# Every block's output is multiplied by the gate as VectorE takes it from PSUM, and gathered rows are added straight into the input rows

## The reference, cut to what matters

```python
    h = rms_norm(x, norm2[l]) * (1.0 + sc2) + sh2
    x = x + g2 * moe_ffn(h, router_w[l], ...)
    return rms_norm(x, norm_f)

def moe_ffn(...):                      # rows sorted by expert into blocks of 128
    def expert_block(args):
        x_blk, e = args
        gu = x_blk @ w_gu[e] + b_gu[e]
        gate = jnp.minimum(gu[:, :D_FF], SWIGLU_LIMIT)
        up = jnp.clip(gu[:, D_FF:], -SWIGLU_LIMIT, SWIGLU_LIMIT)
        act = (up + 1.0) * (gate * jax.nn.sigmoid(SWIGLU_ALPHA * gate))
        return act @ w_down[e] + b_down[e]
    yb = lax.map(expert_block, (xb, block_e)).reshape(rows, D)
    y = jnp.zeros((N, D), h.dtype).at[stok].add(yb[dest] * sg[:, None].astype(h.dtype))
```

## Time and profile before

| | |
|---|---|
| median of three runs | 1630.07 us (1626.98 to 1631.4) |
| profiled execution, its own time | 1626.56 us |
| its span | 1624.6 us |
| busy: PE, DVE, ACT, POOL | 95%, 83%, 60%, 12% of the span |
| mixer and router | about the first 450 us |
| expert blocks | about 450 to 1595 us |
| end: last additions and norm | about 1595 to 1625 us |

### The profile page before, as it was taken

The page is one execution under the profiler, slowest core; times in us unless marked ns, Lnnn a source line. Parts: engine busy times, 40 slices in busy tenths (PEclk is TensorE's granted clock), DMA queues, the critical chain, the costliest instruction groups (busy, mean ns, idle before and its releaser), DMA issues.

```text
span 1624.6 us, 22048 instructions
## 1 busy us (share of the span) xinstructions
PE 1542.7 (95%) x8260; PEld 1163.2 (72%) x8260; DVE 1341.9 (83%) x1048; ACT 979.2 (60%) x787; POOL 187.9 (12%) x210
## 2 busy tenths in 40 slices
PE   3999989998699999999999999999999999999996
PEld 2444358845567787888888888888888888888873
DVE  5557447474878999999999999999999999999987
ACT  4013233311546776777777777777777777777772
POOL 1000121000001110100000100000110000010051
PEclk9999999998789999999999999999999999999998
DMA  9686020242369998999999999999999999999993
GB/s 377 254 343 236 29 91 29 69 168 110 143 258 347 339 390 335 381 388 390 388 380 383 381 380 387 396 391 376 387 379 387 386 395 385 377 388 377 375 379 123
DMA packets 85761, 506.81 MB, mean 312 GB/s; under 512 B 11008, under 2 KB 12336, under 8 KB 33360
## 3 DMA queue, kind: packets, MB, share of 16 engines
q1 hardware_dynamic: 70880, 453.85, 71.5%
q0 software_dynamic: 9104, 34.08, 5.8%
q10 hardware_dynamic: 5728, 18.18, 2.8%
HBM read 477.25 MB, written 28.84 MB: 312 GB/s over the span
## 4 chain that ended last, share of the span: by engine, by line
PE 87%; DVE 7%; DMA 2%; issue 2%; ACT 1%; POOL 1%; SPq 0%; DVEq 0%; POOLq 0%
PE ps L2067 61%; PE ps L1218 8%; PE ps L2083 2%; PE ps L1991 2%; PE ps L1295 2%; PE ps L1120 2%; PE ps L1224 2%; DVE w_lo L1474 2%; PE ps L2046 2%; DMA Wt<-in_ada_w 2%; PE ps L2056 1%; PE ps L1166 1%; PE ps L1193 1%; PE ps L1185 1%; PE ps L2089 0%
## 5 line engine op out<-in xcount | busy, mean ns | idle before, releaser
L1474 DVE TENSOR_TENSOR w_lo<-w_raw,w_hi 128x2048 fp32r<-128x2048 f32 x384 | 864.9, 2287 | 72.5 <-ACT w_hi L1468 72.4
L1468 ACT ACTIVATE w_hi<-w_raw 128x2048 fp32r<-128x2048 f32 x384 | 736.6, 1920 | 291.0 <-PE ps L2067 291.0
L2067 PE MATMUL ps<-w_hi,xTh 128*128 128x512 f32 x1024 | 408.3, 399 | 6.4 <-DVE w_lo L1474 5.8
L2067 PE MATMUL ps<-w_lo,xTh 128*128 128x512 f32 x1024 | 401.6, 392 | 0.0
L2067 PE MATMUL ps<-w_hi,xTl 128*128 128x512 f32 x1024 | 275.7, 391 | 0.0
L2067 PEld LDWEIGHTS ps<-w_hi,xTh 128*128 128x128 f32 x1024 | 194.6, 190 | 60.0 <-issue 16.5
L2067 PEld LDWEIGHTS ps<-w_hi,xTl 128*128 128x128 f32 x1024 | 193.4, 189 | 40.4
L2067 PEld LDWEIGHTS ps<-w_lo,xTh 128*128 128x128 f32 x1024 | 194.3, 190 | 38.5
L2067 PE MATMUL ps<-w_hi,aTh 128*128 128x512 f32 x512 | 202.4, 395 | 0.0
L2067 PE MATMUL ps<-w_lo,aTh 128*128 128x512 f32 x512 | 199.4, 389 | 0.0
L2067 PE MATMUL ps<-w_hi,aTl 128*128 128x512 f32 x512 | 157.6, 389 | 0.0
(11 more groups left out here) (396 smaller groups left out, 1372.3 us busy)
## 6 DMA issues: line engine op xcount, KB each, us to landing
w_raw<-in_moe_w_gu SPq DMA_DIRECT2D x256, 1024.0 KB, 6.6
w_raw<-in_moe_w_down SPq DMA_DIRECT2D x128, 1024.0 KB, 7.0
Wt<-in_ada_w SPq DMA_DIRECT2D x19, 1024.0 KB, 10.4
y_rows<-R ACTq DMA_DIRECT2D x30, 512.0 KB, 6.7
Wt<-in_w_in SPq DMA_DIRECT2D x5, 2048.0 KB, 13.4
y_rows<-Wt POOLq DMA_DIRECT2D x1, 8704.0 KB, 40.7
R<-in_ada_w SPq DMA_DIRECT2D x5, 1024.0 KB, 8.2
R<-in_x SPq DMA_DIRECT2D x2, 2048.0 KB, 10.3
```

The costliest lines, as they stand in the source:

```text
L1468: nc.scalar.activation(w_hi[:, at[-1] % HI_SLOTS, :], w_raw[:, at[-1] % RAW_SLOTS, :], ACT.Copy).then_inc(hi_rdy, 1)
L1474: nc.vector.tensor_tensor(w_lo[:, s, :], w_raw[:, s, :], w_hi[:, at[-1] % HI_SLOTS, :].bitcast(F32), ALU.subtract).then_inc(lo_rdy, 1)
L2067: ins = mm(ps[:, bank0 + c, :], x[:, k, :], w[:, 512 * (banks * i + c):512 * (banks * i + c) + 512], start=(first and i == 0 and x is xh a ...
```

## The change

1. **In the loop.** ACT no longer copies the output of block n-2 out of PSUM. A new function `y_scaled` on DVE, between low halves 3 and 4 of each step (from step 2 on), multiplies banks 6 and 7 by the gate into `ysb[s]`. ACT's `y_store` only waits for it and issues the DMA, in the place where it stood.
2. **Kept blocks.** `y_keep` moves to DVE and multiplies by the gate; for block 31 in two halves of 512 columns, between the adds of tiles 1 and 2. For that PE's last chunk (`last_chunk`) finishes bank 6 before bank 7, and PE's final additions wait per half.
3. **Rows.** As all outputs hold the gate already, `add_row` adds the weighted rows straight into `x2`, all four on DVE; ACT's first-row multiply is gone, and `total` is one addition.
4. **Small.** PE reads the overflow count ahead of the last chunks. ACT runs a one-element root ahead of the final squares. Some semaphores of the mixer and the router are merged (`y_cen` into `y_sum`, `var_mm` into `mean_mm`, `sat_rdy` into `gexp_rdy`, `tail_ev` into `gmt_rdy`).

```diff
-            def y_store(n, s, dn_end, stored, count=None):
-                wait_used(act, dn_end)
-                if stored is not None:
-                    act.wait_ge(y_out[s], 16 * stored)
-                s_.activation(ysb[s].rearrange("p (b c) -> p b c", b=2), ps[:, 6:8, :], ACT.Copy).then_inc(y_ev, 1)
+            def y_store(n, s, count=None):
                 act.wait_ge(y_ev, n + 1 if count is None else count)
                 act.dma_start(y_d[bass.ds(n * BLK, BLK), :], ysb[s]).then_inc(y_out[s], 16)
...
             split_hi(act, place(E, 0))
             split_hi(act, place(E, 1))
-            y_keep(0, place(E - 1, CHUNKS - 1))
             at_evac(E - 1)
             split_hi(act, place(E, 2))
             split_hi(act, place(E, 3))
-            for t in range(TT - 1):
-                act.wait_ge(yg_in[t], 16 * TOPK)
-                s_.activation(yg[t][0], yg[t][0], ACT.Copy, scale=gate_of[:, 0, t, 0:1]).then_inc(first_rdy, 1)
-            y_keep(1, place(E, 3))
...
+            s_.activation(fmx[:, 0:1], epsc[:], ACT.Sqrt)
...
+            def y_scaled(s, dn_end, stored):
+                wait_used(dve, dn_end)
+                if stored is not None:
+                    dve.wait_ge(y_out[s], 16 * stored)
+                v.tensor_tensor(two(ysb[s]), ps[:, 6:8, :], two(mod[5]), ALU.mult).then_inc(y_ev, 1)
+
+            def step(n, where, before, terms=(), done=0, out=None):
                 swiglu(n - 1, before(KT - 1))
                 x_lo(n)
                 for c in range(KT):
+                    if c == 4 and out is not None:
+                        y_scaled(out[0], before(CHUNKS - 1), out[1])
                     if c >= done:
                         split_lo(dve, where(c))
...
+            wait_used(dve, place(E - 1, CHUNKS - 1))
+            y_keep(0, 0, D)
             a_lo(E - 1)
             split_lo(dve, place(E, 2))
             split_lo(dve, place(E, 3))
...
+                return v.scalar_tensor_tensor(out=x2[:, t, :], in0=yg[t][k], scalar=gate_of[:, which, t, k:k + 1],
+                                              in1=x2[:, t, :], op0=ALU.mult, op1=ALU.add)
...
+            add_rows(0)
+            add_rows(1)
+            dve.wait_ge(half_mm, 1)
+            y_keep(1, 0, 512)
+            wait_used(dve, place(E, 3))
+            y_keep(1, 512, D)
+            add_rows(2)
...
-                b = 2 * t
-                if t < TT - 1:
-                    link(v.tensor_tensor(two(yg[t][0]), ps[:, b:b + 2, :], two(yg[t][0]), ALU.add))
-                    into_x(t).then_inc(x3_rdy, 1)
-                else:
-                    link(v.tensor_tensor(two(xg[0]), ps[:, b:b + 2, :], two(mod[5]), ALU.mult))
-                    v.tensor_tensor(x2[:, t, :], x2[:, t, :], xg[0], ALU.add).then_inc(x3_rdy, 1)
+                v.tensor_tensor(two(x2[:, t, :]), ps[:, 2 * t:2 * t + 2, :], two(x2[:, t, :]), ALU.add).then_inc(x3_rdy, 1)
```

More of the change, by code:

```diff
@@ L1636, in _, with step @@
                 split_hi(act, place(1, c))
[L1638 to L1642, removed]
+            def step(n, s, where, before, yn):
                 sigmoid(n - 1, before(KT - 1))
@@ L1647, in step @@
                 if yn is not None:
-                    y_store(yn, s, before(CHUNKS - 1), stored)
+                    y_store(yn, s)
                 for c in range(4, KT):
@@ L1858, in _ @@
             bias_down(0)
-            dve.wait_ge(sat_rdy, 1)
-            def step(n, where, before, terms=(), done=0):
+            dve.wait_ge(gexp_rdy, 3)
+            def y_scaled(s, dn_end, stored):
[4 more added lines that the diff above has]
+            def step(n, where, before, terms=(), done=0, out=None):
                 swiglu(n - 1, before(KT - 1))
@@ L1902, in _ @@
             step(1, at_step(1), at_step(0), ((1, 2), (2, 7)), EARLY)
-            step(2, at_step(2), at_step(1), ((3, 7),))
-            for n in (3, TT):
-                step(n, at_step(n), at_step(n - 1))
+            step(2, at_step(2), at_step(1), ((3, 7),), out=(0, None))
+            step(3, at_step(3), at_step(2), out=(1, None))
+            step(TT, at_step(TT), at_step(TT - 1), out=(0, 1))
             tail_rows()
@@ L1954, in _ @@
                 for t in range(TT - 1):
-                    link_over(v.tensor_scalar(yg[t][0], yg[t][0], gate_of[:, 1, t, 0:1], None, ALU.mult))
-                    for k in range(1, TOPK):
+                    for k in range(TOPK):
                         link_over(add_row(t, 1, k))
@@ L2071, in chunk, with last_chunk @@
                 ins.then_inc(w_used, 1)
+            def last_chunk(at):
+                hs, ls = at[-1] % HI_SLOTS, at[-1] % RAW_SLOTS
+                wait_made(pe, lo_rdy, at)
+                for c in range(2):
+                    for i in range(2):
+                        w = slice(512 * (2 * i + c), 512 * (2 * i + c) + 512)
+                        mm(ps[:, 6 + c, :], aTh[:, KT - 2 + i, :], w_hi[:, hs, w], start=False, stop=False)
+                        mm(ps[:, 6 + c, :], aTh[:, KT - 2 + i, :], w_lo[:, ls, w], start=False, stop=False)
+                        ins = mm(ps[:, 6 + c, :], aTl[:, KT - 2 + i, :], w_hi[:, hs, w], start=False, stop=(i == 1))
+                    if c == 0:
+                        ins.then_inc(half_mm, 1)
+                ins.then_inc(w_used, 1)
             def gate_up(at, c):
@@ L2166, in _ @@
             tail_add(2, 0, True, False)
-            for c in range(4):
+            ov = overflow_count(pe)
+            for c in range(3):
                 down(place(E, c), c)
-            ov = overflow_count(pe)
+            last_chunk(place(E, 3))
             with pe.If(ov > 0):
-                pe.wait_ge(y_last, 2)
+                pe.wait_ge(y_last, 3)
                 for t in range(TT - 1):
@@ L2191, in _, with tail_half @@
                 pe.wait_ge(tail_new, TOPK)
-            pe.wait_ge(y_last, 2)
+            def tail_half(t, i, c, bank, start, stop):
+                return mm(ps[:, bank + c, :], tailT[:, i, P * t:P * t + P], y_tail[i][:, 512 * c:512 * c + 512],
+                          start=start, stop=stop)
             for t in range(TT - 1):
-                tail_add(t, 1, False, True).then_inc(fin_mm, 1)
+                for c in range(2):
+                    pe.wait_ge(y_last, 2 + c)
+                    ins = tail_half(t, 1, c, 2 * t, False, True)
+                ins.then_inc(fin_mm, 1)
             t = TT - 1
-            tail_add(t, 0, True, False)
-            tail_add(t, 1, False, False)
+            for i in range(2):
+                for c in range(2):
+                    tail_half(t, i, c, 2 * t, i == 0, False)
             pe.wait_ge(yg_in[t], 16 * TOPK)
```

54 lines of the change are left out of this document (23 added, 31 removed).

## The result

| | before | changed |
|---|---|---|
| median | 1629.6 us, 4 runs (1626.98 to 1631.4) | 1657.69 us, 4 runs (1654.93 to 1658.29) |
| profiled execution, its own time | 1626.56 us | 1657.82 us |
| its span | 1624.6 us | 1655.7 us |

The ratio is 1.0172, with a 95% interval of 1.0155 to 1.0188: the change makes the kernel 28 us slower. The two profiled spans differ by more, 31.1 us, since the profiled execution of before was shorter than each of its four runs.

A forecast was written before the change was run, and what follows sets the result against it. TensorE bounds the loop before (35.39 us per block), VectorE after (36.29). Loop +26.1 and tail -0.8 give +25.3 us on the profiled 1626.56, so 1651.9; the median lies 3.5 higher: 1655.4 us (1646 to 1665).

The forecast's parts named there:

- The room, 2.92 us: In the expert loop, VectorE's own work takes 32.47 us of a 35.39 us block, leaving 2.92 us.
- The multiply holds 1.14 us: In the loop, VectorE's new multiply of two PSUM banks by the gate holds the engine 1.14 us per block.
- The handover, 2.68 us: In the loop, ScalarE's store waits for VectorE's multiply, delaying the fifth high half; VectorE idles 2.68 us (2.55 to 2.81).
- +0.90 us per block: In the loop, VectorE's round becomes 36.29 us, 0.90 more than TensorE's (0.77 to 1.03).
- TensorE waits once per block, at the fifth chunk, 0.8 to 1.0 us: In the loop, some 29 TensorE waits of 0.8 to 1.0 us for a low half, one per block.
- The clock costed at nothing: TensorE's waits of 0.9 us should leave its clock at 2.4 GHz, so no cost was added.
- 29 blocks that pay: Of thirty stored blocks in the loop, 29 pay 0.90 us each: +26.1 us (22.3 to 29.9).
- The tail, -0.8 us: At the kernel's end, several small moves together save 0.8 us (from -1.5 to +1).
- step (a): In the tail, kept block 30 leaves PSUM on VectorE behind two low halves; its twelve matmuls start 2.0 us later.
- the first (the room holds): Rival for the loop: a waiting store does not hold later high halves, loop unchanged, 1629.3 us; chance 0.09.
- The second, the clock falling at each wait: Rival for TensorE in the loop: 2.4 us lost per block, at most 70 us, total 1700; chance 0.03.
- The third, a dearer handover: Rival for the loop: multiply or handover dearer, each 0.1 us per block adding 2.9 us, 1667 at 0.4; chance 0.03.

The follow-up runs named there:

- the loop repaired: The changed kernel with ScalarE's store of the block's output moved behind the high halves of chunks 4 to 7: 1627.06 us, ratio 0.9986.
- the two repairs of the loop: The changed kernel with ScalarE's store behind the high halves of chunks 4 to 7 (1627.06 us), or with VectorE's multiply one low half earlier (1627.02 us).
- the work alone: The kernel before with one extra VectorE multiply per block at the place of the new one, nothing waiting for it: 1630.69 us, ratio 1.0016.
- the wait alone: The kernel before, its copy still on ScalarE, with the store's DMA also waiting for VectorE's fourth low half: 1628.6 us, ratio 1.0003.
- both repairs: The changed kernel with ScalarE's store behind its eighth high half and VectorE's kept copies moved earlier in the tail: 1626.39 us, ratio 0.9988.
- more work: The changed kernel with one extra VectorE multiply per block ahead of the seventh low half: 1688.43 us, ratio 1.0363.
- the tail alone: The changed kernel with VectorE's kept copies ahead of the second low half and of the eighth row add, loop untouched: 1654.2 us, ratio 1.0156.
- the entry's store later: The changed kernel with ScalarE's store behind the eighth high half in steps 2 and 3 only: 1654.22 us, ratio 1.0156.
- the run with two multiplies: The kernel before with two extra VectorE multiplies per block ahead of the fifth low half, nothing waiting for them: 1627.76 us, ratio 0.9994.
- the run with three multiplies: The kernel before with three extra VectorE multiplies per block, two ahead of the fifth low half, one within the activation: 1644.21 us, ratio 1.0087.

## Why the prediction was right, and where it was not

It said 1655.4 us (1646 to 1665), slower with 0.90. Measured: 1657.69. Its steps:

- **The room, 2.92 us.** Shown: 2 x 1.14 is free, 3 x 1.14 adds 0.49 per block.
- **The multiply holds 1.14 us.** Shown: the next instruction starts 1.13 after it does, and in a loop without room one more costs 1.135.
- **The handover, 2.68 us (2.55 to 2.81).** VectorE's next low half starts at 927.05 where its multiply would have let it at 924.38: 2.67. The parts are as priced: 0.18 to the issue, 0.34 for it, 0.13 to the next activation. The step that no trace of before could show, that a waiting store holds the activations behind it, is shown by the wait put in alone.
- **+0.90 us per block.** It was 0.94, inside the 0.77 to 1.03. Over the 26 blocks from the sixth to the last activation VectorE fell 24.4 us behind where 23.4 were forecast.
- **TensorE waits once per block, at the fifth chunk, 0.8 to 1.0 us.** Not so: it waits at the fifth chunk and at the first. From the first chunk's start to the fifth's it takes 929.40 - 916.77 = 12.63 us against 12.06 before, so 0.57 there; the other 0.37 stands at the first chunk, whose low half comes last as well. The sum is that forecast.
- **The clock costed at nothing.** Right for the loop (1.00), wrong at its ends, and this is the step that failed. In the changed kernel's profile it cost 1.7 us in the tail and most of 4.6 in steps 1 to 3. In step 2 a wait of the length that before had left the clock at 1.00 was followed by a stretch at the lower level (last section).
- **29 blocks that pay.** It was 26. The start of TensorE's bias matmuls in each block tells by how much TensorE falls behind the kernel before: 0.27 us by the second block, then 1.05 in step 1, 1.58 in step 2, 1.98 in step 3, 1.13 in step 4, nothing in steps 5 and 6, and 23.4 in the 25 steps from 7 on, 0.94 each. The handover is paid in step 4 and from step 7 on, 24.5 us in all where 26.1 were forecast. In steps 2 and 3, as slow as they are by the clock, it adds nothing: with the store later they take the same time. Steps 5 and 6 take TensorE no longer than before, though the sixth and the seventh activation of VectorE are already 36.37 us apart instead of 35.38.
- **What steps 1 to 3 lost, 4.6 us.** The clock, for the most part. Step 1, which the change doesn't touch, begins in every kernel with a wait of 3.17 or 3.18 us; over the 5 us behind it the clock was 0.50 in the changed kernel and 0.66 before. From the first activation to the second it took 39.14 us in the changed kernel against 38.10; the two versions with the same 0.50 took 39.09 and 39.12, the nine others, at 0.66 to 0.70, 37.9 to 38.6. In steps 2 and 3 the clock fell once each, 1.7 us of work, where before it did not, and in step 3 the wait itself was 1.98 us against 1.63.
- **The tail, -0.8 us.** From TensorE's transposes to the last scaling it takes 1647.18 - 1606.08 = 41.10 us against 39.48 before: +1.6, outside the -1.5 to +1. Its step (a) had the matmuls on the kept block 2.0 us later; they came 1.76 later against TensorE (the wait 1.93 for 0.17). What it left out is the slow clock behind that wait, 1.7 us; without it the tail would be 39.4 long, which is -0.1. The overflow count's load and the table load cost nothing: TensorE has no gap ahead of its last chunks, and the table loads at 1611.87 in an idle stretch of ScalarE. With the loop repaired the same tail is 38.44 us long (1616.30 - 1577.86, its transposes' start), 1.0 shorter than before, but its wait for the kept block is 0.92 instead of 1.93, so that it does not test the -0.8 for the changed loop.

Together, against the profiled execution: 0.3 ahead of step 1, 4.6 in steps 1 to 3, 24.5 of handover and 1.6 in the tail, 31.0 of the 31.1 us of span, where +25.3 were forecast. Against the median, whose runs of before lie higher than the profiled one, it is 28.1. The nearness of the total owes something to luck: the three blocks counted too many (2.7 us) stood against some 6 us of clock that had been left out, and the profiled execution of before lay 3 us under its median. Of the rivals, the first (the room holds) is not what the changed kernel does, but it became true with either of the two repairs of the loop. The second, the clock falling at each wait, did not happen, even with twice the waits. The third, a dearer handover, fell with the measured 2.67.

What stays open is why the clock fell in steps 2 and 3 of the changed kernel and not before. The run made for it shows only that the store is not the cause: with it later the clock fell there too.

## What to carry to other kernels

Write down for each engine of a loop its own round (the sum of what its instructions hold it, without waits), and subtract from the period: the remainder is the room, and it pays for added work and for added waits from the same purse. A busy share shows the work but not the waits, so it can fall while the engine becomes the bound. Before an instruction that waits is moved onto a queue, or its signal moved to a slower giver, read what stands behind it on that queue and who waits for that; here moving one DMA issue behind four activations, or its giver ahead of one, recovered all of the loss.

## What the runs showed of the hardware

Whether TensorE's clock falls after a short wait isn't decided by the wait's length. In the third and the fourth block (steps 2 and 3) TensorE waits for the first low half in every one of the twelve kernels. In the third block that wait is 1.62 to 1.64 us in eleven of them. Behind it the clock kept its 1.00 in six (before, and the runs with the store later, the multiply earlier, the work alone, the wait alone and both repairs) and fell in five (the changed kernel, its versions with more work, with the tail alone and with the entry's store later, and the run with two multiplies). TensorE's first 5 us behind the wait, in the kernel before:
```profile
505.80:510.80 5.00, 5.00 (x22) 1.00 1.07 398
```
in the changed kernel:
```profile
507.13:512.13 5.00, 5.00 (x15) 0.66 0.74 313
```
and, in the run with three multiplies, behind its waits of 2.69 us in the third block and again 2.69 in the fourth:
```profile
506.30:511.30 5.00, 5.00 (x16) 0.69 0.82 333
...
548.06:553.06 5.00, 5.00 (x22) 1.00 0.89 334
```
So 1.63 us can cost the clock and 2.69 us can leave it. Where it fell behind a wait of 1.62 to 1.64 us, it did to a mean of 0.66 over 5 us, which is 0.34 x 5 = 1.7 us of work lost, the same as behind the 1.93 us in the tail. In the fourth block waits of 1.63 us left the clock in two kernels (before, and the wait alone) and cost it in two (two multiplies, and the changed kernel with more work), and all seven of 1.98 or 1.99 us cost it. In the tails 1.82, 1.92 and 2.31 us left it at 1.00, and 1.93 and 2.99 cost it. Waits of TensorE of these lengths, 1.6 to 3 us, should be priced at themselves plus nothing or 1.7 us, with both ends in the range; the waits of up to 1.5 us in the loops from 900 to 1500 never cost more than themselves.
